# The first norm and w_v's first eight tiles in two halves of 512 features, with w_v's and w_u's low tiles made whole on VectorE

## What is computed

```python
mod_lat = jnp.split((jax.nn.silu(c) @ ada_w[i] + ada_b[i])[:, None, :], MOD_CHUNKS, axis=-1)
h_lat = _modulate(x_lat, norm1_g[i], mod_lat[0], mod_lat[1])      # rmsnorm(x, gain) * (1 + scale) + shift
z = _gelu(h @ w_in)
u, v = z[..., :SGU_WIDTH], z[..., SGU_WIDTH:]
v = _rmsnorm(v, v_gain)                                            # then mixed over the tokens of a chunk
y = (u * sv) @ w_out
x_lat = x_lat + mod_lat[2] * y_lat
```

## Time and profile before

| | us |
|---|---|
| three runs | 1923.33, 1925.81, 1928.08 |
| their median | 1925.81 |
| the profiled execution | 1926.24 |
| its span in the trace | 1924.4 |
| mean granted clock of TensorE in it | 0.992 |

### The profile page before, as it was taken

How to read it: one execution, slowest core, us unless ns; L and a number is a source line. 1 busy time by engine, 2 the same in 40 slices (tenths; PEclk the granted TensorE clock), 3 DMA queues, 4 the chain that set the end, 5 groups by cost and what they waited for, 6 DMA issues and landing times.

```text
span 1924.4 us, 38569 instructions
## 1 busy us (share of the span) xinstructions
PE 1891.0 (98%) x13356; PEld 1694.0 (88%) x13356; DVE 1527.0 (79%) x2601; ACT 924.4 (48%) x1484; POOL 407.0 (21%) x205
## 2 busy tenths in 40 slices
PE   6999999999999999999999999999999999999998
PEld 6999999998888888888889899999888878888887
DVE  6876599957998888888886569994898888886555
ACT  3464444545555544444445444454555544444444
POOL 1544468820000000000003358870000000000000
PEclk8999999999999999999999999999999999999999
DMA  8855445555544445478883345455554454545553
GB/s 320 323 200 204 137 166 181 178 184 208 208 174 168 172 173 174 174 269 320 323 299 121 110 165 175 175 185 188 206 209 166 171 174 172 172 173 191 190 194 131
DMA packets 104182, 376.43 MB, mean 196 GB/s; under 512 B 12464, under 2 KB 12464, under 8 KB 103856
## 3 DMA queue, kind: packets, MB, share of 16 engines
q1 hardware_dynamic: 103680, 373.43, 54.6%
q0 software_dynamic: 432, 2.10, 0.3%
HBM read 374.43 MB, written 1.05 MB: 195 GB/s over the span
## 4 chain that ended last, share of the span: by engine, by line
PE 55%; issue 18%; POOL 15%; DMA 4%; DVE 4%; ACT 2%; SPq 1%; POOLq 0%; DVEq 0%; ACTq 0%
PE O L1530 12%; PE O L1532 12%; PE O L1531 12%; POOL wL L405 9%; PE ring L1496 7%; POOL wL L392 6%; PE ring L1498 4%; DMA raw<-in_u 3%; PE ring L1240 2%; PE ring L1241 2%; PE ring L1242 2%; ACT wH L434 2%; DVE wL L691 2%; PE ring L1472 2%; PE O L1472 1%
## 5 line engine op out<-in xcount | busy, mean ns | idle before, releaser
L434 ACT ACTIVATE wH<-raw 128x1024 fp32r<-128x1024 f32 x608 | 645.0, 1061 | 915.5 <-DMA raw<-in_v 376.8
L691 DVE TENSOR_TENSOR wL<-raw,wH 128x1024 fp32r<-128x1024 f32 x416 | 509.4, 1225 | 238.1 <-ACT wH L434 232.2
L1240 PE MATMUL ring<-hX,wH 128*128 128x256 f32 x1512 | 433.0, 286 | 5.3 <-DVE wL L679 3.8
L1241 PE MATMUL ring<-hX,wH 128*128 128x256 f32 x1512 | 427.6, 283 | 0.0
L1242 PE MATMUL ring<-hX,wL 128*128 128x256 f32 x1512 | 427.6, 283 | 0.0
L1530 PE MATMUL O<-wH,gateH 128*128 128x512 f32 x1024 | 406.5, 397 | 0.8 <-DVE gateL L1122 0.4
L1532 PE MATMUL O<-wH,gateL 128*128 128x512 f32 x1024 | 400.0, 391 | 0.0
L1531 PE MATMUL O<-wL,gateH 128*128 128x512 f32 x1024 | 398.8, 389 | 0.0
L1496 PE MATMUL ring<-hX,wH 128*128 128x512 f32 x1024 | 367.5, 401 | 0.0
L1240 PEld LDWEIGHTS ring<-hX,wH 128*128 128x128 f32 x1512 | 289.8, 192 | 7.6 <-POOL wL L405 2.7
L1241 PEld LDWEIGHTS ring<-hX,wH 128*128 128x128 f32 x1512 | 290.0, 192 | 0.1
(11 more groups left out here) (177 smaller groups left out, 2167.7 us busy)
## 6 DMA issues: line engine op xcount, KB each, us to landing
raw<-in_u SPq DMA_DIRECT2D x256, 512.0 KB, 3.4
raw<-in_v SPq DMA_DIRECT2D x256, 512.0 KB, 3.5
ada_v<-in_ada SPq DMA_DIRECT2D x40, 512.0 KB, 4.9
raw<-in_w_in SPq DMA_DIRECT2D x32, 512.0 KB, 4.4
raw<-in_w_q SPq DMA_DIRECT2D x32, 512.0 KB, 3.5
ada_s<-in_ada SPq DMA_DIRECT2D x20, 512.0 KB, 5.1
ada_f<-in_ada SPq DMA_DIRECT2D x16, 512.0 KB, 11.1
raw<-in_w_out SPq DMA_DIRECT2D x16, 512.0 KB, 3.5
```

The lines of the kernel that those rows point to most:

```text
L434: nc.scalar.activation(wH[s % RAW][:, :], raw[s % RAW][:, :], ACT.Copy).then_inc(s_h, 1)
L691: nc.vector.tensor_tensor(wL[s % RAW][:, :], raw[s % RAW][:, :], wH[s % RAW][:, :].bitcast(fp32), ALU.subtract).then_inc(s_low, 1)
L1240: mm(bank[:, 0:T], a, xH[:, k0 + k, :], start=(first and k == 0), stop=False)
L1241: mm(bank[:, 0:T], a, xL[:, k0 + k, :], start=False, stop=False)
```

## The change

Before, all 1024 features of norm 0 had to be ready before the first product. In the changed kernel the norm and the first eight w_v tiles are done in two halves, features 0 to 511 and 512 to 1023.

- The host packs the first 16 ada tiles so that tiles 0 to 7 hold shift and scale of features 0 to 511, tiles 8 to 15 those of the other features (`ada_tiles`). It packs w_v's first eight tiles so that each 512 KB holds two output tiles for four k only (`front_tiles`).
- SyncE loads XT first, then the eight ada tiles and four weight tiles of each half. The weight tiles of the second half wait for the first half's slots.
- A `front_slot` of TensorE is 24 matmuls into the two halves of one bank. The sums of slots 0 to 3 stay in the four banks until slots 4 to 7 add the other features to them. Only then does ScalarE empty each bank, two feature tiles at a time.
- VectorE's order is: eight ada tiles (the inverse root after the sixth), low tile 0, the first half's modulations and h, low tiles 1 to 3 alternating with ada tiles 8 to 10, ada tiles 11 to 13, low tile 4, the second half's modulations and h, low tiles 5 to 9. The last two ada tiles are not added by VectorE: `front_sums` on TensorE multiplies them by silu(c) together with the column of ones for the sum of the others.
- In the whole of w_v and w_u VectorE makes low tiles of 1024 columns, and GpSimd starts with w_out.
- The ada tiles of `ada_s` are loaded in pairs behind w_v's tiles 12 to 15, and with each of w_u's first twelve; VectorE adds eight in w_v (steps 8 to 15) and twelve in w_u.

The diff, cut to what is told of here; "..." marks what is left out:

```diff
...
         ADA_SLOTS = tuple(s for s in range(12) if s % 3 < 2)
-        ADA_W_V = tuple(t for t in range(16) if t % 4 < 3)
+        FRONT_AT = (8, 9, 10, 11, 0, 1, 2, 3, 4, 5, 6, 7, 12, 13, 14, 15)
+        FRONT_SUMMED = ADA_FRONT - 2
         ADA_W_OUT = (4, 5, 7, 8)
...
                 sp.dma_start(dst, src).then_inc(s_first, 16)
-            for m in range(ADA_FRONT):
-                sp.dma_start(ada_f[m][:, :], ada_d[(m + KT) % ADA_FRONT]).then_inc(s_front[m], 16)
-                if m == KT - 1:
-                    sp.dma_start(XT[:, :, :], xt_d).then_inc(s_x, 16)
-            for t in range(RAW):
-                load(stream_dram["w_v", 0], 0, 0, t, first=True)
+            sp.dma_start(XT[:, :, :], xt_d).then_inc(s_x, 16)
+            for half in range(2):
+                for m in range(half * KT, half * KT + KT):
+                    sp.dma_start(ada_f[FRONT_AT[m]][:, :], ada_d[m]).then_inc(s_front[m], 16)
+                for r in range(4):
+                    load(stream_dram["w_v", 0], 0, half, r, first=(half == 0))
             for dst, src in small_loads:
...
             m = ADA_FRONT
-            for t in range(16):
-                if t >= RAW:
-                    load(stream_dram["w_v", 0], 0, t // 4, t % 4)
-                if t in ADA_W_V:
+            for t in range(8, 16):
+                load(stream_dram["w_v", 0], 0, t // 4, t % 4)
+                if t > 11:
                     load_ada(ada_s, m)
-                    m += 1
+                    load_ada(ada_s, m + 1)
+                    m += 2
             for t in range(16):
                 load(stream_dram["w_u", 0], W_U, t // 4, t % 4)
-                if t < 8:
+                if t < 12:
                     load_ada(ada_s, m)
...
-            def front_low(s):
-                pool.wait_ge(s_h, s + 1)
-                nc.gpsimd.tensor_tensor(wL[s][:, 0:HALF], raw[s][:, 0:HALF], wH[s][:, 0:HALF].bitcast(fp32),
-                                        ALU.subtract).then_inc(s_first_l, 1)
             pool.wait_ge(s_acc, ADA_FRONT)
...
                 if layer == 0:
-                    front_low(0)
-                    front_low(1)
-                    low_second(0, 0, 2, 3)
-                    low_second(0, 0, 3)
-                with pool.Fori(1 - layer, (end - base) // 4) as i:
+                    low_second(W_OUT, 0, 0, W_OUT + 1)
+                    for s in range(1, 4):
+                        low_second(W_OUT, 0, s)
+                with pool.Fori((W_OUT // 4 + 1) * (1 - layer), (end - base) // 4) as i:
                     for s in range(4):
...
                 root(n)
-                if n == 0:
-                    for s in range(3):
-                        split_high(0, 0, s)
-                    act.wait_ge(s_mod, 2)
                 if n < NORMS - 1:
...
             act.wait_ge(s_const, 6)
-            norm(0)
+            root(0)
+            for half in range(2):
+                split_high(0, half, 0)
+                split_high(0, half, 1)
+                for k in range(4 * half, 4 * half + 4):
+                    act.wait_ge(s_xn, k + 1)
+                    nc.scalar.activation(hH[:, k, :], sq[:, k, :], ACT.Identity, bias=modcol(0, 0, k, 1)).then_inc(s_hH, 1)
+                split_high(0, half, 2)
+                split_high(0, half, 3)
             for layer in range(LAYERS):
...
                     warm()
-                    with act.Fori(0, 16 // 4) as i:
+                    for r in range(4):
+                        act.wait_ge(s_pe, 5 + r)
+                        nc.scalar.activation(UV[:, SGU_FT + 2 * r:SGU_FT + 2 * r + 2, :].rearrange("p a t -> p (a t)"),
+                                             ring[r][:, :], ACT.Gelu).then_inc(s_bank_a, 2)
+                        if r < 3:
+                            split_high(0, 2, r)
+                    with act.Fori(2, 16 // 4) as i:
                         for s in range(4):
...
+                width = D if base < W_OUT and base + 4 * i + s < W_OUT else HALF
                 dve.wait_ge(s_h, 4 * i + (base + s + 1))
-                nc.vector.tensor_tensor(wL[s % RAW][:, 0:HALF], raw[s % RAW][:, 0:HALF],
-                                        wH[s % RAW][:, 0:HALF].bitcast(fp32), ALU.subtract).then_inc(s_l0, n)
-            def front_rest(s):
-                dve.wait_ge(s_h, s + 1)
-                nc.vector.tensor_tensor(wL[s][:, HALF:], raw[s][:, HALF:], wH[s][:, HALF:].bitcast(fp32),
-                                        ALU.subtract).then_inc(s_first_r, 1)
+                nc.vector.tensor_tensor(wL[s % RAW][:, 0:width], raw[s % RAW][:, 0:width],
+                                        wH[s % RAW][:, 0:width].bitcast(fp32), ALU.subtract).then_inc(s_l0, n)
+            def low_front(i):
+                dve.wait_ge(s_h, i + 1)
+                nc.vector.tensor_tensor(wL[i % RAW][:, :], raw[i % RAW][:, :], wH[i % RAW][:, :].bitcast(fp32),
+                                        ALU.subtract).then_inc(s_l0, 1)
...
                 dve.wait_ge(s_front[m], 16)
-                add_ada(acc_f, m // KT, ada_f[m], m, m % KT)
+                add_ada(acc_f, m // KT, ada_f[FRONT_AT[m]], m, m % KT)
...
             dve.wait_ge(s_silu, 1)
-            for m in range(KT + 3):
+            def front_modulations(half):
+                def columns(of):
+                    return of[:, 0:2 * KT].rearrange("p (c h j) -> p h c j", c=2, h=2)[:, half]
+                dve.wait_ge(s_modp, half + 1)
+                sums = O[3][:, half * KT:half * KT + KT].rearrange("p (c j) -> p c j", c=2)
+                after(step(nc.vector.tensor_tensor(columns(mod), sums, columns(adab), ALU.add)))
+                after(step(nc.vector.scalar_tensor_tensor(gs[:, 0, 4 * half:4 * half + 4], modcol(0, 1, 4 * half, 4), 1.0,
+                                                          n1[:, 4 * half:4 * half + 4], ALU.add, ALU.mult)))
+            def front_half(half):
+                front_modulations(half)
+                dve.wait_ge(s_rstd, 1)
+                scaled(0, 4 * half)
+                scaled(0, 4 * half + 1)
+                for k in range(4 * half, 4 * half + 4):
+                    low_h(0, k)
+                    if k % 4 < 2:
+                        scaled(0, k + 2)
+            for m in range(KT):
                 ada_front(m)
-            modulations(1, (1,), O[3], (0,))
-            for m in range(KT + 3, ADA_FRONT):
-                ada_front(m)
-                if m == ADA_FRONT - 2:
+                if m == 5:
                     inverse_root(0)
             dve.wait_ge(s_x, 16)
-            dve.wait_ge(s_rstd, 1)
-            for k in range(4):
-                scaled(0, k)
-            modulations(2, (0,), O[3][:, KT:], ())
-            front_rest(0)
-            for k in range(KT):
-                if k < 4:
-                    scaled(0, k + 4)
-                low_h(0, k)
-                if k == 1:
-                    front_rest(1)
+            low_front(0)
+            front_half(0)
+            for i in range(1, 4):
+                low_front(i)
+                ada_front(KT + i - 1)
+            for m in range(KT + 3, FRONT_SUMMED):
+                ada_front(m)
+            low_front(4)
+            front_half(1)
+            nc.vector.memset(tick[:, 0:1], 0.0).then_inc(s_mod, 2)
+            nc.vector.memset(tick[:, 5:6], 0.0).then_inc(s_acc, ADA_FRONT - FRONT_SUMMED)
+            for i in range(5, 8):
+                low_front(i)
+            low_first(W_V, 2, 0)
+            low_first(W_V, 2, 1)
             for layer in range(LAYERS):
...
                     m = ADA_FRONT
-                    for t in range(16):
-                        low_first(W_V, t // 4, t % 4 + 2, 1 if t else 3)
-                        if t in ADA_W_V:
-                            ada_tile(ada_s, acc_s, m // KT - 2, m)
-                            m += 1
+                    for t in range(8, 16):
+                        low_first(W_V, t // 4, t % 4 + 2)
+                        ada_tile(ada_s, acc_s, m // KT - 2, m)
+                        m += 1
...
                         ahead(W_U, t // 4, t % 4)
-                        if t < 8:
+                        if t < 12:
                             ada_tile(ada_s, acc_s, m // KT - 2, m)
...
                 for k in range(KT):
-                    if whole is None and by_pool is None and k % 4 == 0:
+                    if whole is None and by_pool is None and k % 4 == 0 and (k == 0 or base >= W_OUT):
                         pe.wait_ge((s_l0, s_l1)[k // 4], 4 * i + (base - HALVES[base >= BASE["p_in", 1]] + s + 1))
...
                 def weights(half, tiles):
-                    if n == 0:
-                        pe.wait_ge((s_first_l, s_first_r)[half], 2)
-                    else:
-                        pe.wait_ge((s_l0, s_l1)[half], base - HALVES[base >= BASE["p_in", 1]] + tiles)
+                    pe.wait_ge((s_l0, s_l1)[half], base - HALVES[base >= BASE["p_in", 1]] + tiles)
...
```

(72 more changed lines are left out.)

7 lines of the change are left out of this document (2 added, 5 removed).

## The result

| | before | after |
|---|---|---|
| median of 20 runs each, us | 1925.18 | 1927.77 |
| ratio, 95% interval | 1 | 1.0019 [1.0012, 1.0027] |
| span of the profiled execution, us | 1924.4 | 1924.5 |
| first load of w_out issued, us | 132.99 | 136.22 |

The time lies in the forecast range and under 0.3% from before, but on the other side: 0.4 us less was forecast, and the ratio says 0.0019 * 1925 = 3.7 us more (the medians, 2.6). The two profiled spans are equal to 0.1 us, so they don't carry this comparison. The last row does: SyncE issues w_out's first load when the thirteenth product of w_u is done. It is the **landmark** of all that follows. It moved by 3.2 us, and the two kernels then take the same 54.6 us from there to the first load of the next stage's weights (187.57 before, 190.82 after).

What follows compares the result with a forecast made beforehand. TensorE, busy 98% of the span, was taken as the bound. The terms 23.7 + 15.6 + 7.8 + 14.8 + 23.0 + 1.5 gave 86.4 against 86.8, 0.4 us earlier: 1925.4 us, range 1919.8 to 1931.0.

Steps and rivals of the forecast that it cites:

- M: Date at which the first half's modulations are made: 23.7 us, with ends 23.0 and 26.3.
- first half, M to the sums: From M until VectorE reaches the 14th ada addition, with slots 0 to 3 run meanwhile: 15.6 us.
- the sums: TensorE's 48 column-sum instructions for the second half, 26 at full clock and 22 at half: 7.8 us.
- second half: Second half's modulations to its eighth product: 14.1 us as the first, plus 0.7 for a partly hidden half-clock slot, 14.8.
- tiles 8 to 15 with the stall: w_v's other eight tiles, 23.0 us, plus 1.5 for TensorE's stall at tile 11 behind VectorE's wait for ada_s.
- end of w_v: Sum of all terms up to w_v's last product: 86.4 us against 86.8 in the kernel before.
- w_u, stalls in its first tile: No stall was forecast at w_u's start, costed at 0; TensorE was to be full through w_u.
- What w_u and all behind it need stays as it is: From w_v's end on nothing changes, so a shift there reaches the kernel's end whole; costed at nothing.
- rival C: VectorE's queue becomes the bound in w_u steps 8 to 13: 3 us more, 1928.4; chance 0.10.
- rival B: Half clock from the sums' start and through most of slot 5: 4.5 us more, 1929.9; chance 0.17.
- the full windows give the whole tiles nothing: TensorE full from 70 to 150 us, so ending GpSimd's halves in w_v and w_u gains and costs nothing.
- the cover that I named: In w_u, idle waits of 2.67 and 1.56 us and 3.1 from ended contention cover VectorE's added work.

Runs made afterwards that it cites:

- g1_ada_ahead: Changed kernel, four ada_s tiles loaded ahead of w_v's tile 8, then one behind each of w_v's 13 to 15 and w_u's 0 to 12: 1922.84 us.
- f1_ada_ahead: Changed kernel, four ada_s tiles loaded ahead of w_v's tile 8, then one behind each of w_v's 10 to 15 and w_u's first ten: 2011.49 us.
- e2_sums_vector: Changed kernel with all sixteen front ada tiles added by VectorE, the second half's column sums 16 instructions instead of 48: 1923.44 us, 0.9991 of the kernel before.
- f3_sums_and_clock: Changed kernel with all sixteen additions on VectorE and keep_clock calls, 12 ahead of the second column sums and 4 behind: 1921.85 us, 0.9992 of before.
- g4_before_whole: Kernel before with only VectorE's whole low tiles from w_v's tile 2 through w_u, GpSimd starting with w_out: 1923.04 us, 0.9988 of before.
- e4_gpsimd_back: Changed kernel with GpSimd again making the second 512 columns of low tiles from w_v's tile 8 and in w_u: 1929.53 us, 1.0026 of before.
- e1_ada_one_each: Changed kernel with one ada_s tile issued behind each of w_v's tiles 8 to 15 instead of pairs behind 12 to 15: 1927.16 us, 1.0014 of before.
- g2_all_three: g1_ada_ahead with the edits of e2_sums_vector and f3_sums_and_clock: 1918.07 us, 0.9962 of the kernel before.
- g3_fewer_calls: g2_all_three with 5 keep_clock calls instead of 12 ahead of the first column sums: 1922.43 us, 0.9986 of the kernel before.
- e3_clock_between: Changed kernel with one keep_clock call between each two of the second half's eight column sums, 14 more instructions: 1931.46 us, 1.0037 of the kernel before.

## Why the prediction missed the sign

| step | forecast | measured | error |
|---|---|---|---|
| M | 23.7 | 23.41 | -0.3 |
| first half, M to the sums | 15.6 | 14.9 | -0.7 |
| the sums | 7.8 | 8.6 | +0.8 |
| second half | 14.8 | 15.6 | +0.8 |
| tiles 8 to 15 with the stall | 24.5 | 25.1 | +0.6 |
| end of w_v | 86.4 | 87.55 | +1.15 |
| w_u, stalls in its first tile | 0 | 0.71 + 1.34 | +2.05 |

**The step that failed** is "What w_u and all behind it need stays as it is". Its price was nothing, and w_u lost 2.05 us in two waits and about 0.4 in restarts. I took w_u as full and looked there for VectorE's load alone (rival C). SyncE's queue I followed for the first ada pair only, and stopped at its landing. The change puts eight ada loads among the four last weight loads of w_v, and each from the fifth on waits for an addition. A wait on SyncE holds every weight load behind it, and I never asked what stands behind those. That g1_ada_ahead takes the stalls away with the same work and the same bytes in another order shows it, and f1_ada_ahead shows how far the same ring can go. The sum up to the end of w_v was 1.15 us short besides, 86.4 for 87.55, and that alone would have turned 0.4 less into 0.7 more. That it wasn't worse is luck: the first two terms, 1.0 us too long, hid half of the 2.2 that the next three were short.

**The terms.** The start was right to 0.3, first product at 25.02 as written. The first half was 0.7 shorter: 0.5 of it because the first addition of a chunk has nothing to add to. It takes 0.75, or 0.66 to the next start, which a row (19.31) shows, and stood in the sum at 1.2; the other 0.2 came in the chain of hL. The sums were a size off in the right mechanism: the clock fell at about 40.3, after 18 of the 48 instructions instead of 26: 18 * 0.115 + 30 * 0.218 = 8.6, not 7.8. The second half was at half clock to 54, all of slot 4 and not a part of one slot: +0.8. This is rival B in its place, but not its point of decision, since slot 5 ran mostly at full clock. The wait of VectorE for ada_s was there (5.00 us before 70.53), and TensorE's at tile 11 was 1.30 for the forecast 1.5; the other 0.75 of tiles 8 to 15 is restart and gaps too short to be listed as waits. The prediction also took 0.3% for what a measurement can tell; the interval of 20 runs each was 0.08% to either side, and so the 0.19% is a change, and slower.

**The clock.** The prediction weighed the Trainium skill (TensorE: Matmul & The Clock Gate, HAM oscillation), by which bursts with waits between them start throttled. The runs agree where a wait is filled or not: 3.38 us idle and half clock behind it in e2_sums_vector, 1.00 throughout in f3_sums_and_clock. They show one more thing: in after only 0.60 us of idle time came ahead of the sums, and the clock still fell, while one-column instructions kept the engine busy in the profile's sense. Whether that short wait or the 48 instructions did it isn't separated: f3_sums_and_clock, which kept the clock, changed both.

**GpSimd.** That the full windows give the whole tiles nothing was wrong twice. In w_v the waits of 1.93 us were VectorE's under contention, and g4_before_whole takes 1.5 of them. In w_u the cover that I named (3.1 us back from contention) is what kept rival C from happening; e4_gpsimd_back is rival C in its place (w_u's steps 10 to 12) and near its price, 3.7 us at the landmark for 3, though through the modulations that the mixing waits for, which I hadn't named. By the Trainium skill (GPSIMD Engine Reference, section 1, Specifications) alone the stage would gain; here the 1.5 us of g4_before_whole agree with that rule, and my objection to it fell.

**What stays open.** Why the weight tiles took 6.2 us to land in after and 3.7 in g1_ada_ahead isn't taken apart. Two ada tiles just ahead in the queue, at 1.29 us each, would make 2.6, and one 1.3; e1_ada_one_each took 5.4 with one ada load ahead, as g1_ada_ahead has, so it isn't that alone. Why the clock falls behind the means in most runs and in some not, which moves M between 22.3 and 24.8, isn't known either. Behind the landmark the profiled execution of after gained its 3.2 us back by the end, while the medians of 20 runs didn't. The traces show where: at the start of layer 0's channel mixer the granted clock fell in the kernel before and not in after, and at the first load of the experts' weights (246.91 and 248.96) 2.05 us are left of the 3.2. Windows from 200 to 210, before and after:

```profile
200.00:210.00 10.00, 9.97 (x71) 9.77 (x71) 7.03 (x20) 5.09 (x11) 0.00 (x0) 0.86 0.01 2
```
```profile
200.00:210.00 10.00, 9.91 (x83) 9.60 (x83) 6.34 (x19) 5.12 (x12) 2.45 (x2) 1.00 0.16 52
```

Another 0.9 us of idle time in 540 to 560 stands in before alone (busy 19.11 of 20 us, 20.00 in after). The fall near 200 is in the traces of g2_all_three, g3_fewer_calls, g4_before_whole and e4_gpsimd_back too, and in those of e1 to e3, f3_sums_and_clock and g1_ada_ahead it isn't. So it isn't tied to the old start or the new one, and one execution of each tells no more; why it comes isn't known.

## What to carry to other kernels

When loads move in a queue that works in order, write down for each load that waits who raises its semaphore, and what stands behind it; a load that waits for compute must not stand ahead of one that feeds the same compute, unless what it waits for is long done. Four places filled ahead took that wait away for nothing where the next ada loads came three tiles behind what they waited for (g1_ada_ahead), and with the next ones earlier cost 84 us (f1_ada_ahead). An engine given more work may live on contention that ends elsewhere, so try the two halves of such a change apart. If TensorE has to wait ahead of short instructions, dense calls in the wait kept its clock here; calls strewn between the short ones didn't.

## What the hardware did that I had not expected

- The clock fell while 32-bit matmuls of one column ran back to back: 0.115 us each up to 40.3, 0.22 behind it, and with a pair of full-width instructions among every six (e3_clock_between) only some 2 us later.
- After such a stretch the clock came back 5.6 us after slot 4's start in after (48.42; 0.50 at 53 to 54, 1.00 at 54 to 55), and 4.0 after it in e2_sums_vector (45.13; 0.71 from 48 to 50, 1.00 behind). The same work under the same clock got it back at different dates.
- The start, too, is not the same each time: the 24 instructions ahead of the first sums took 2.84 us in g1_ada_ahead, 3.79 in after and 5.17 in g2_all_three, with the clock at 1.00 from 12 to 20 in the first and at 0.50 from 14 to about 20, or to 22, in the others. That is the spread of M.
- DMA shares of 0.97 to 1.02 from 70 to 82 us cost TensorE nothing in g1_ada_ahead.
- Ada loads placed one step too early on SyncE made a tile take 8.4 us instead of 2.88 or 3.3 for 15 tiles on end: the pipeline didn't recover until the ada loads ended.
